# Two fused transformer blocks in fp32, split into high and low parts: every fourth low part of the second feed-forward block made by ScalarE and an accumulating DMA

## The reference, cut to what matters

```python
h = rmsnorm_2(x, norm_ffn[i])
up = dwconv3(h @ ffn_w_up[i], ffn_conv_w[i], ffn_conv_b[i])
gate, val = jnp.split(up, 2, axis=-1)
x = x + (jax.nn.silu(gate) * val) @ ffn_w_down[i]
```

## Time and profile before

| what | value |
|---|---|
| median of 3 runs | 2586.16 us (2585.28 to 2586.39) |
| span of the profiled execution | 2583.9 us |
| TensorE busy | 2575.3 us (100%) |
| VectorE busy | 1898.9 us (73%) |
| ScalarE busy | 1472.9 us (57%) |
| GpSimd busy | 318.0 us (12%) |
| moved by DMA | 493.71 MB, mean 191 GB/s |

### The profile page before, as it was taken

One profiled execution on the slowest core, in us unless ns is written; L12 is line 12 of the kernel. 1 busy time (PEld: TensorE's weight loads), 2 busy tenths in 40 slices (PEclk: granted clock), 3 DMA queues, 4 the chain that ended last, 5 costly groups with the idle time before them and its releaser, 6 DMA issues.

```text
span 2583.9 us, 37523 instructions
## 1 busy us (share of the span) xinstructions
PE 2575.3 (100%) x14624; PEld 2243.1 (87%) x14624; DVE 1898.9 (73%) x2868; ACT 1472.9 (57%) x2247; POOL 318.0 (12%) x292
## 2 busy tenths in 40 slices
PE   9999999999999999999999999999999999999998
PEld 8888888888889888888888888888888888888887
DVE  7787777777977876666666698788876766667675
ACT  6666657776656544444444466445654545555554
POOL 2111103316201010101000043101100000000000
PEclk9999999999999999999999999999999999999999
DMA  7565666566656566666666656556666666666665
GB/s 247 179 221 187 188 200 199 177 206 189 210 174 197 168 188 189 191 190 188 194 187 190 191 185 223 160 171 191 189 198 189 192 191 189 193 190 194 189 190 160
DMA packets 137353, 493.71 MB, mean 191 GB/s; under 512 B 15448, under 2 KB 16345, under 8 KB 136793
## 3 DMA queue, kind: packets, MB, share of 16 engines
q1 hardware_dynamic: 136600, 490.80, 62.0%
q10 hardware_dynamic: 576, 0.53, 0.1%
HBM read 489.14 MB, written 2.13 MB: 190 GB/s over the span
## 4 chain that ended last, share of the span: by engine, by line
PE 100%; DMA 0%; ACT 0%; DVE 0%; issue 0%; ACTq 0%
PE ps L978 57%; PE ps L975 28%; PE ps L950 4%; PE ps L948 4%; PE ps L949 4%; PE ps L992 0%; PE ps L1107 0%; PE ps L963 0%; PE ps L964 0%; PE ps L965 0%; PE ps L1199 0%; PE ps L938 0%; PE ps L936 0%; PE ps L937 0%; PE ps L1108 0%; PE ps L1059 0%
## 5 line engine op out<-in xcount | busy, mean ns | idle before, releaser
L978 PE MATMUL ps<-X,wh 128*128 128x512 f32 x4752 | 1590.8, 395 | 0.7 <-DVE X L1588 0.7
L1582 DVE TENSOR_TENSOR wl<-raw,wh 128x1024 fp32r<-128x1024 f32 (+1 forms) x908 | 1149.0, 1268 | 503.0 <-ACT wh L1224 502.3
L1224 ACT ACTIVATE wh<-raw 128x1024 fp32r<-128x1024 f32 (+1 forms) x908 | 955.3, 1054 | 728.2 <-PE ps L975 553.5
L975 PE MATMUL ps<-X,wl 128*128 128x256 f32 x4752 | 1199.3, 278 | 0.0
L978 PEld LDWEIGHTS ps<-X,wh 128*128 128x128 f32 x4752 | 863.0, 188 | 170.8 <-issue 2.2
L975 PEld LDWEIGHTS ps<-X,wl 128*128 128x128 f32 x4752 | 872.1, 188 | 37.9
L978 PE MATMUL ps<-XG,wh 128*128 128x512 f32 x1472 | 492.0, 394 | 0.0
L975 PE MATMUL ps<-XG,wl 128*128 128x256 f32 x1472 | 371.6, 278 | 0.0
L978 PEld LDWEIGHTS ps<-XG,wh 128*128 128x128 f32 x1472 | 266.9, 188 | 53.1 <-issue 0.9
L1224 ACT ACTIVATE T<-ps 128x256 f32<-128x256 f32 x444 | 145.8, 380 | 252.2 <-PE ps L975 250.3
L975 PEld LDWEIGHTS ps<-XG,wl 128*128 128x128 f32 x1472 | 269.7, 188 | 11.3
(11 more groups left out here) (237 smaller groups left out, 1614.6 us busy)
## 6 DMA issues: line engine op xcount, KB each, us to landing
raw<-in_w_gate SPq DMA_DIRECT2D x176, 512.0 KB, 3.8
raw<-in_w_down SPq DMA_DIRECT2D x176, 512.0 KB, 3.7
raw<-in_w_sc SPq DMA_DIRECT2D x95, 512.0 KB, 4.3
raw<-in_w_up SPq DMA_DIRECT2D x88, 512.0 KB, 3.7
raw<-in_w_val SPq DMA_DIRECT2D x88, 512.0 KB, 3.7
raw<-in_w_zx SPq DMA_DIRECT2D x80, 512.0 KB, 3.9
raw<-in_w_in SPq DMA_DIRECT2D x56, 512.0 KB, 3.7
raw<-in_w_osc SPq DMA_DIRECT2D x32, 512.0 KB, 4.1
```

The costliest lines, as they stand in the source:

```text
L975: t = e.matmul(bank(c, i)[:, 0:256], wl[:, b0:b0 + 128], X[:, kx * 512:kx * 512 + 256], start=False, stop=sp and kk == c.kn - 1)
L978: e.matmul(bank(c, i)[:, :], wh[:, b0:b0 + 128], X[:, kx * 512:kx * 512 + 512], start=st and kk == 0, stop=False)
L1224: return e.activation(out, in_, ACT.Copy, scale=scale)
L1582: return e.tensor_tensor(out, a, b, op)
```

## The change

In the second feed-forward block, from its first `w_gate_2` unit (638) to twelve units before the end, the units with u % 4 = 2 get their low part in another way. There are 63 of them: 44 are the first unit of a gate or value column, 19 are `w_down_2` units. For such a unit ScalarE, right behind the copy to `wh`, copies `raw` once more with the factor -1.0 to `wl` (rounded in the same way, so it is the negated high part). GpSimd waits for that and issues a DMA that reads the raw slot and adds it to the `wl` slot, in place. VectorE's subtraction of that unit is gone. TensorE's wait for the unit, and SyncE's wait before the load of unit u + 4, go to the completion of that DMA. Semaphores are renamed and merged to make room (`mmv` into `mm0`, `s_pad` into `s_ones`, and `neg` is the earlier `tsq`). Nothing else is moved.

```diff
+ADDED = [u for u in range(next(c for c in COLS if c.src == "w_gate_2").first, NU - 12) if u % 4 == 2]
...
+def subtracted(u):
+
+    return halves(u) - len([k for k in ADDED if k <= u])
+
+
+def low_part(w, lo, d_lo, u):
+
+    if u in ADDED:
+        k = ADDED.index(u)
+        w.wait_ge(d_lo[k % 2], 16 * (k // 2 + 1))
+    else:
+        w.wait_ge(lo, subtracted(u))
...
+    neg, d_lo = tsq, [sem(f"d_lo{i}") for i in range(2)]
...
             if u >= NRAW:
-                w.wait_ge(lo, halves(u - NRAW))
+                low_part(w, lo, d_lo, u - NRAW)
             e.dma_start(raw[:, r * UN:(r + 1) * UN], T_[col.src][col.c, g]).then_inc(d_raw[r], 16)
...
             if u > 1:
-                w.wait_ge(lo, halves(u))
+                low_part(w, lo, d_lo, u)
...
                     copy(wh[:, b * UN:(b + 1) * UN], raw[:, r * UN:(r + 1) * UN]).then_inc(hi, 1)
+                    if i in ADDED:
+                        copy(wl[:, b * UN:(b + 1) * UN], raw[:, r * UN:(r + 1) * UN], -1.0).then_inc(neg, 1)
...
-                if piece == "split":
+                if piece == "split" and i not in ADDED:
                     r, b = i % NRAW, i % NW
                     w.wait_ge(hi, halves(i))
...
+                if piece == "split" and i in ADDED:
+                    r, b, k = i % NRAW, i % NW, ADDED.index(i)
+                    w.wait_ge(neg, k + 3)
+                    e.dma_start(wl[:, b * UN:(b + 1) * UN].bitcast(F32), raw[:, r * UN:(r + 1) * UN], accum_op=ALU.add).then_inc(d_lo[k % 2], 16)
```

More of the change, by code:

```diff
@@ L561, in program @@
     d_out = [sem(f"d_out{i}") for i in range(3)]
-    hi, lo, mm, mm0, mmv = sem("hi"), sem("lo"), sem("mm"), sem("mm0"), sem("mmv")
+    hi, lo, mm, mm0 = sem("hi"), sem("lo"), sem("mm"), sem("mm0")
     evA, evD, evS, cvA, cvV = (sem(n) for n in ("evA", "evD", "evS", "cvA", "cvV"))
@@ L575, in program @@
     sq2, acc2, fold2, nmm2, fA, fv, hA, hP = (sem(n) for n in ("sq2", "acc2", "fold2", "nmm2", "fA", "fv", "hA", "hP"))
-    s_ones, s_pad, s_gg, vc = (sem(n) for n in ("ones", "pad", "gg", "vc"))
+    s_ones, s_gg, vc = (sem(n) for n in ("ones", "gg", "vc"))
     d_tok, tsq, nbc, ntr, nrs = [sem(f"d_tok{i}") for i in range(2)], sem("tsq"), sem("nbc"), sem("ntr"), sem("nrs")
+    neg, d_lo = tsq, [sem(f"d_lo{i}") for i in range(2)]
     snb, snt, snc = (sem(n) for n in ("snb", "snt", "snc"))
@@ L954, in unit @@
                 if u == U_V and halves_[-1] == 0:
-                    t.then_inc(mmv, 1)
+                    t.then_inc(mm0, 1)
             elif c.src == "w_o":
@@ L1347, in scalar @@
                     for st in range(2):
-                        w.wait_ge(*((mm, NU) if st else (mm0, 1)))
+                        w.wait_ge(*((mm, NU) if st else (mm0, 2)))
                         w.wait_ge(sq, 45 + st)
@@ L1360, in scalar @@
                 if piece == "vcopy":
-                    w.wait_ge(*((mm, U_V + 1) if i else (mmv, 1)))
+                    w.wait_ge(*((mm, U_V + 1) if i else (mm0, 1)))
                     w.wait_ge(nv, 10)
@@ L1478, in scalar @@
                     else:
-                        w.wait_ge(s_pad, 1)
+                        w.wait_ge(s_ones, 2)
                     copy(srs(i), sbank(i)[:, 256:512]).then_inc(snc, 1)
@@ L1741, in vector @@
                         for n in range(2):
-                            w.wait_ge(*((mm, NU) if n else (mm0, 1)))
+                            w.wait_ge(*((mm, NU) if n else (mm0, 2)))
                             k = 14 + n
@@ L2143, in gpsimd @@
         e.memset(ones[:, :], 1.0).then_inc(s_ones, 1)
-        e.memset(Rt[:, :], 0.0).then_inc(s_pad, 1)
+        e.memset(Rt[:, :], 0.0).then_inc(s_ones, 1)
         def add(out, a, b, op=ALU.add):
```

## The result

| | median | runs |
|---|---|---|
| before | 2585.66 us | 10 runs, 2584.65 to 2586.56 |
| changed | 2592.54 us | 10 runs, 2590.91 to 2596.99 |

The ratio is 1.0028, with a 95% interval of 1.0019 to 1.0037: the change costs 6.9 us. The forecast was 2621 us. The profiled execution is the slowest of the ten, 2596.99 us, so its trace shows more than the 6.9 us.

The account below looks back on a forecast made before the run. TensorE was taken as the bound; 22 us from 44 column turns and 13 us from 19 down turns gave 35 us on 2583.9, so 2619, and with 2.3 us for the runs' median 2621 us; 8-in-10 range 2584 to 2700.

Parts of the forecast that it names:

- TensorE sets the pace, VectorE's relief is worth nothing: Second feed-forward block: TensorE is busy throughout, so removing 63 VectorE subtractions, 77 us in all, gains nothing.
- ScalarE's second copy costs nothing beside the path: 63 added ScalarE copies, 67 us, are covered by its idle time; on the unit's own path they count.
- x = 5.6 us: Time from GpSimd's release to the accumulating DMA's landing, bounded from neighbouring transfers and taken as 5.6 us.
- the prediction's own signs: Stated tests: wrong if the transfer lands in under 4.9 us or its unit loads take longer than 3.7 us.
- The sum: Turns of 11.6 us: 0.5 over in 44 column turns, 0.7 over in 19 down turns, 35 us in all.
- The second loop: Slot of raw: copies, transfer and next load make a turn of x + 6.0 us, binding from x = 4.9 to 5.1.
- the first loop: Slot of wl: TensorE waits for the unit only if x is over 5.8 us; slack falls to 0.2 us.
- Three loads go out together behind the held one: SyncE's queue: three loads go out with the held one, needed 2.8, 5.5 and 8.3 us later, not late themselves.
- Hidden: Rival: x is 4.9 us or less, the transfer is covered by the wait for TensorE's slot, 2586 us; 36%.
- Long transfer: Rival: x is 6.7 to 7.8 us from engines shared with loads or slow GpSimd issue, 2691 to 2760 us; 21%.
- Faster: Rival: TensorE gets quicker because VectorE reads and writes less, at most 1.7 us to gain; 1%.

Follow-up runs that it names:

- e4: Changed kernel with neither DMA nor subtraction at the 63 units; TensorE and SyncE wait for ScalarE's negated copy: 2585.48 us against 2585.41 before.
- e8: Changed kernel without the DMA: the 63 units get ScalarE's extra copy, then VectorE's subtraction as before: 2586.46 us against 2585.34 before.
- e5: Changed kernel, but GpSimd's DMA copies the raw unit over the wl slot instead of adding it: 2585.52 us against 2585.34 before.
- e9: Changed kernel, but the accumulating DMA reads the unit from HBM (types fp32r), next load still held until it lands: 2632.25 us against 2585.83 before.
- e2: Changed kernel with every fifth unit (u % 5 = 2) through the DMA instead of every fourth: 2586.89 us against 2585.41 before.
- e6: Changed kernel with only every eighth unit (u % 8 = 6) through the DMA: 2586.06 us against 2585.34 before.
- e10: Changed kernel, but in SyncE's queue the load waiting for the DMA stands behind the next load: 2654.89 us against 2585.83 before.
- e12: Changed kernel, but ScalarE writes the negated copy in eight pieces, the last releasing GpSimd: 2611.74 us against 2585.60 before.
- e3: Changed kernel, but the DMA reads the unit from HBM (types fp32r) and the next load waits only for ScalarE's copies: 2715.45 us against 2585.41 before.
- e7: Changed kernel with every second unit (even u) through the DMA: 2733.31 us against 2585.34 before.
- e1: Changed kernel, but ScalarE writes the negated copy before the high part, releasing the DMA earlier: 2588.67 us against 2585.41 before.

## Why the prediction was wrong in size

**TensorE sets the pace, VectorE's relief is worth nothing.** Right: e4 and e8, within 1.1 us.

**ScalarE's second copy costs nothing beside the path.** Right by the same runs. On the path it was 2.12 us in my sum and is 2.01, since the second copy starts 0.97 us after the first.

**x = 5.6 us.** This is the step that failed, in size. Measured: 5.18 us on average from ScalarE's end, 4.87 in the middle, 6.5 at most. Its kind was right, a transfer and a second stream of reads. Both parts were too high. For the first I took a load, 3.7 us; the plain copy of e5 takes 3.4 in the middle from ScalarE's end. For the second I took 1.8 us, the engine time of a load in its 2.77 us; it costs 8 packets x 0.18 us = 1.4 (e5). A load's packets of 4096 bytes take 217 ns on average in the kernel before (159 in the middle), those of the plain copy on the chip 161, and 8 x 217 ns is the 1.8. Why some packets of a load are slow is not shown. The 1024 KB rows, both loads from HBM, were too high a neighbour too; with HBM as the source x is 5.9 (e9). The estimate from the Trainium skill, "DMA: Bandwidth & Descriptors", Anatomy of one DMA, SWDGE (gpsimd) path, 4.4 us, is near the 4.6 in the middle from issue to landing; the 0.3 us from ScalarE's end to GpSimd's start and the long transfers come on top of it. By the prediction's own signs it is wrong twice: 34 of the 63 x are under 4.9 us, and the unit loads take more than 3.7.

**The sum.** With x at its measured average the same sum gives 0.08 x 44 + 0.28 x 19 = 9 us in place of 35, so the wrong x alone accounts for nearly all of the error: 0.4 us in one term made the result about five times too large. That 9 is so near to the 9.4 of the trace and the 6.9 of the runs is in part luck, since the sum multiplies a constant. In fact x and the load vary from turn to turn: 14 of the 63 DMAs take over 5.5 us from ScalarE's end, and at 9 others the held load takes over 4.4 us. Such turns are over the limit, the others are under it and catch up. The mean turn was 11.27 us and not 11.6, and the stalls are 15, not about 60.

**The second loop is the tighter one and binds.** Half right. 42 waits of ScalarE end at loads, e2 and e6 undo it, e10 and e12 deepen it. But a turn at the median x is 2.0 + 4.87 + 3.7 + 0.1 = 10.7 us, under TensorE's 10.9 to 11.1, so the limit of x was 5.1 to 5.3 and not 4.9 to 5.1; and 3.3 of the 7.9 us of stalls come from the first loop alone, which the prediction had left with 0.2 us to spare.

**Three loads go out together behind the held one.** They do not: they follow it by 0.4, 0.9 and 3.5 us in the middle, the last one after a wait for VectorE's low part. None of them makes a high part late, as forecast. But the last of them is still in flight when the next accumulating DMA starts, and every one of the 63 has a load beside it, which the prediction did not count.

**Rivals.** Hidden: nearly so, at 2592.5 instead of 2586; it needed x under 4.9 each time, and had it at 34 of the 63. Long transfer: not in this kernel; only e3 has such an x, 7.7 us. e7 is as slow with an average of 5.9. I had put the DMA share at up to 0.96 and it is 0.77: over 1960 to 2540 the new queue takes 24.6%, and the loads' own share goes down from 63.2 to 52.1%. Faster: no.

What stays open: why one accumulating DMA is long and the next is not. Across kernels x grows with the time that loads run beside it, but within the changed kernel that time hardly tells the 14 long ones (2.4 us) from the others (2.1 us). Long and short ones come in runs and in alternation, and the ten times of the changed kernel spread over 6 us where those of before spread over 2. A fifth raw slot, which would give the loop more room, was not tried.

## What to carry to other kernels

When a step of a buffer's round is replaced by a longer one, add up the whole turn (copy, transfer, landing, next load) and compare it with the turn of the engine that sets the pace: here 11.27 against 11.11 us decided, and work taken from an engine that is not the bound gave nothing. Close to that limit state the loss as a slope: here 0.1 us in a turn is 6 us in the program, so a range must follow from the uncertainty of each term. Look at the spread of a transfer too, not only at its average: single long ones stall the engine where the average doesn't. Don't send the same slot through the slow path each time: a stride of five in place of four, at a depth of four, hid four fifths as many transfers.

## What the runs showed of the hardware

- An accumulating DMA from on-chip memory to on-chip memory takes twice as long for each packet as a plain copy (340 against 160 ns for 4096 bytes); 512 KB land 4.6 us after GpSimd's issue instead of 3.2, and the issue itself occupies GpSimd for 0.86 instead of 0.53 us (changed kernel and e5).
- With HBM as the added operand's source (and fp32r as the type) it is 5.6 us with the loads held back (e9) and 7 to 8 us with the loads running (e3).
- A load that goes out 1.4 us behind another takes 5.2 us to land, one that goes out first 3.9 us (e10 and the changed kernel).
- Starting the transfer 1.0 us earlier made it 0.6 us longer (e1): near other traffic, a shorter path is not a shorter turn by as much.
